# The first gate and up product of a transformer's FFN multiplied as a pair, with six slots of split weights and a ring of five

## The reference

```
mod = silu(c) @ ada_w + ada_b;  sh1, sc1, g1, sh2, sc2, g2 = split(mod, 6)
h = rms_norm(x, norm1_g) * (1 + sc1) + sh1
proj = h @ w_in + b_in                 # u, lru_gate, q, k, v, mix_gates
merged = gate_lru * (y_lru @ w_lru_out) + gate_attn * (y_attn @ w_attn_out)
x = x + g1 * (merged @ w_o)
h2 = rms_norm(x, norm2_g) * (1 + sc2) + sh2
gate, up = split(h2 @ w_ffn_in, 2)     # w_ffn_in: 2048 x 2*5632
x = x + g2 * ((silu(gate) * up) @ w_ffn_out)
x = rms_norm(x, final_g)
```

## Time and profile before

| | |
|---|---|
| median of 3 runs | 2730.45 us (2726.79 to 2730.5) |
| profiled execution: its time, its span | 2728.78, 2727.0 us |
| granted TensorE clock, mean | 0.997 |
| PE busy | 2688.0 us (99%) |
| DVE, ACT, POOL busy | 1889.8 (69%), 1317.2 (48%), 30.2 us (1%) |
| moved | 598.60 MB, mean 220 GB/s |
| chain that ended last | PE 89%, DVE 4%, DMA 3%, ACT 2% |

### The profile page before, as it was taken

One profiled execution on the slowest core, in us unless ns is written; L12 is line 12 of the kernel. 1 busy time (PEld: TensorE's weight loads), 2 busy tenths in 40 slices (PEclk: granted clock), 3 DMA queues, 4 the chain that ended last, 5 costly groups with the idle time before them and its releaser, 6 DMA issues.

```text
span 2727.0 us, 34023 instructions
## 1 busy us (share of the span) xinstructions
PE 2688.0 (99%) x13322; PEld 2258.8 (83%) x13322; DVE 1889.8 (69%) x2563; ACT 1317.2 (48%) x1874; POOL 30.2 (1%) x60
## 2 busy tenths in 40 slices
PE   8999999999999999999999999999999999999998
PEld 5888888888888788888888888888888888888886
DVE  7868777778886665554554477778587757765775
ACT  4158665544444644344434456554465434443443
POOL 0100000000000000000000000000000000000000
PEclk9999999999999999999999999999999999999999
DMA  9964657799987786555555555543555555555553
GB/s 363 409 256 155 220 198 262 266 344 351 329 278 235 232 271 215 194 191 192 186 193 191 194 181 187 176 146 133 197 196 188 192 193 186 190 193 194 188 191 125
DMA packets 161832, 598.60 MB, mean 220 GB/s; under 512 B 18151, under 2 KB 18376, under 8 KB 160392
## 3 DMA queue, kind: packets, MB, share of 16 engines
q1 hardware_dynamic: 154824, 564.71, 61.1%
q0 software_dynamic: 6848, 31.72, 3.0%
HBM read 592.17 MB, written 4.19 MB: 219 GB/s over the span
## 4 chain that ended last, share of the span: by engine, by line
PE 89%; DVE 4%; DMA 3%; ACT 2%; issue 1%; POOL 0%; SPq 0%; DVEq 0%; ACTq 0%
PE PS L681 88%; DMA W<-in_ada_first 2%; DVE ACC L1966 1%; DVE WL L1963 1%; DMA W<-in_w_mix 1%; ACT WH L1320 1%; PE PS L902 0%; PE PS L1099 0%; DMA W<-in_ada 0%; DVE G L1963 0%; DVE XB L1963 0%; DVE TT L1963 0%; DVE G L1966 0%; DMA W<-in_w_lru_out 0%; ACT L1546 0%
## 5 line engine op out<-in xcount | busy, mean ns | idle before, releaser
L1963 DVE TENSOR_TENSOR WL<-W,WH 128x1024 fp32r<-128x1024 f32 x876 | 1068.5, 1223 | 639.1 <-ACT WH L1320 637.6
L1320 ACT ACTIVATE WH<-W 128x1024 fp32r<-128x1024 f32 x876 | 924.5, 1058 | 818.5 <-PE PS L681 742.8
L681 PE MATMUL PS<-XA,WH 128*128 128x512 f32 x2480 | 799.6, 399 | 2.3 <-DVE WL L1963 1.6
L681 PE MATMUL PS<-WH,XA 128*128 128x512 f32 (+1 forms) x2560 | 797.1, 390 | 4.7 <-DVE XA L1963 4.3
L681 PE MATMUL PS<-WH,XB 128*128 128x512 f32 x1952 | 611.7, 391 | 0.0
L681 PEld LDWEIGHTS PS<-WH,XA 128*128 128x128 f32 x2560 | 479.3, 188 | 104.8 <-DVE XA L1963 5.9
L681 PEld LDWEIGHTS PS<-XA,WL 128*128 128x128 f32 x2480 | 466.2, 188 | 106.5 <-issue 0.7
L681 PE MATMUL PS<-WL,XA 128*128 128x512 f32 (+1 forms) x1280 | 495.7, 387 | 0.0
L681 PE MATMUL PS<-XA,WL 128*128 128x256 f32 x2480 | 491.8, 278 | 0.0
L681 PEld LDWEIGHTS PS<-WH,XB 128*128 128x128 f32 x1952 | 366.4, 188 | 76.1 <-issue 0.7
L681 PEld LDWEIGHTS PS<-XA,WH 128*128 128x128 f32 x2480 | 384.8, 189 | 6.1 <-DVE WL L1963 2.7
(11 more groups left out here) (231 smaller groups left out, 1333.6 us busy)
## 6 DMA issues: line engine op xcount, KB each, us to landing
W<-in_w_ffn_in SPq DMA_DIRECT2D x176, 512.0 KB, 4.2
W<-in_w_up SPq DMA_DIRECT2D x176, 512.0 KB, 3.8
W<-in_w_in SPq DMA_DIRECT2D x132, 512.0 KB, 4.2
W<-in_ada SPq DMA_DIRECT2D x128, 512.0 KB, 5.4
W<-in_w_ffn_out SPq DMA_DIRECT2D x88, 512.0 KB, 3.7
W<-in_w_down SPq DMA_DIRECT2D x88, 512.0 KB, 3.6
W<-in_ada_first SPq DMA_DIRECT2D x64, 512.0 KB, 9.2
W<-in_w_mix SPq DMA_DIRECT2D x64, 512.0 KB, 5.5
```

Of the source, the lines that this page charges most:

```text
L681: return e.matmul(o, l, r, start=start, stop=stop, skip_group_check=True)
L1320: return e.activation(o, a, ACT.Copy)
L1963: return e.tensor_tensor(o, a, b, op)
```

## The change

- `PAIR` = ("fg", 0) and ("fu", 0), multiplied by the new `moving_pair`: token half 0 of k tiles 0 to 3 for the one and then for the other, with the turn of token half 1 after the second k tile of the other; then token half 1 of the four for each; then k tiles 4 to 7 of the one, 4 to 7 of the other, and so on. `ring_plan` loads the weights in this order.
- USLOTS 4 to 6, RING 6 to 5 (12 raw slots at the start instead of 8). The two take 12 KB more of each partition, and the scratch for GpSimd's descriptors is cut from 16384 to 4096 bytes.
- ScalarE does the conversions of rest[0] and rest[1] before the first copies; VectorE does the one of rest[1] after the scaling of token half 1, and splits the residual of half 1 in two steps between the low parts. Both have one conversion for each of k tiles 4 to 15 then. ScalarE does two of the pair's conversions after the Silu of ("fg", 0).

```
-RING = 6
-USLOTS = 4
+RING = 5
+USLOTS = 6
...
         for h in c[::4]:
-            w += [("w_ffn_in", a + h + i) for a in (0, NHID) for i in range(4)]
+            if h == 0:
+                w += [("w_ffn_in", a + i) for i in range(4) for a in (0, NHID)]
+            else:
+                w += [("w_ffn_in", a + h + i) for a in (0, NHID) for i in range(4)]
...
+        def moving_pair(keys, X, name, turn_half, make):
...
             held = []
+            for key in keys:
+                free_bank(key)
+                for kt in range(EARLY):
+                    w.wait_ge(*xl[name, kt, 0])
+                    held += tiles(key, [kt])
+                    _, _, whi, wlo, _ = held[-1]
+                    three(key, X, kt, 0, whi, wlo, kt == 0, False)
+                    if key == keys[1] and kt == EARLY // 2 - 1:
+                        for j in range(EARLY // 2):
+                            turn_half(j, 1)
+            for n, (kt, key, whi, wlo, names) in enumerate(held):
                 w.wait_ge(*xl[name, kt])
+                m = three(key, X, kt, 1, whi, wlo, kt == 0, False)
                 if names:
                     m.then_inc(*mm(*names))
+                if n in (1, 3):
+                    make("begin", EARLY + n - 1)
+            for k in range(EARLY, KT, EARLY):
+                for key in keys:
+                    for kt in range(k, k + EARLY):
...
+                        three(key, X, kt, 0, whi, wlo, False, last)
+                        m = three(key, X, kt, 1, whi, wlo, False, last)
...
+                        if key == keys[0] and kt % 2 and kt + 3 < KT:
+                            make("begin", kt + 3)
...  scalar
         boundary(rest[0])
-        h2_half(0, (0, 1))
         boundary(rest[1])
-        h2_half(0, (2, 3))
+        h2_half(0, range(EARLY))
...
-        group([("fg", 0)], modulated, EARLY)
+        for i, u in enumerate(BEGIN[PAIR[0]][:PAIR_STEPS]):
+            if EARLY + i < KT:
+                modulated("begin", EARLY + i)
+            boundary(u)
...
+                if c == 0:
+                    for u in BEGIN[PAIR[0]][PAIR_STEPS:]:
+                        boundary(u)
...  vector
         boundary(rest[0])
-        h2_low(0, (0, 1))
-        residual(key, 3, ROW1, (1,))
-        boundary(rest[1])
+        h2_low(0, (0,))
+        gated(key, 3, ROW1, 1)
+        h2_low(0, (1,))
+        gated_in(key, 3, (1,))
+        h2_low(0, (2, 3))
         add_parts("r1", 1)
-        h2_low(0, (2, 3))
         invert("r1", 1)
         w.wait_ge(*iv["r1", 1])
         share(0, 1)
+        boundary(rest[1])
         shares(1)
         h2_low(1, (0, 1))
         boundary(rest[2])
         h2_low(1, (2, 3))
...
-    nc = bacc.Bacc("TRN2", target_bir_lowering=False, num_devices=1)
+    nc = bacc.Bacc("TRN2", target_bir_lowering=False, num_devices=1, dynamic_dma_scratch_size=4096)
```

More of the change, by code:

```diff
@@ L258 @@
 EARLY = 4
-GROUPS = [[("u", o) for o in range(NU)], [("gg", 0), ("gu", 0), ("gg", 1), ("gu", 1)]]
+PAIR = [("fg", 0), ("fu", 0)]
+PAIR_STEPS = 14
+GROUPS = [[("u", o) for o in range(NU)], PAIR, [("gg", 0), ("gu", 0), ("gg", 1), ("gu", 1)]]
 IN_GROUP = {k for g in GROUPS for k in g}
@@ L794, in moving, with tiles @@
                     between(i)
-        def moving_ramp(key, X, name, turn_half, make):
+        def moving_pair(keys, X, name, turn_half, make):
+            def tiles(key, kts):
+                return [(kt, key, *columns(width(key))) for kt in kts]
             held = []
[L799 to L811, removed]
-                w.wait_ge(*xl[name, kt])
[L813 to L819, removed]
@@ L820, in moving_ramp @@
                 if names:
                     m.then_inc(*mm(*names))
+                if n in (1, 3):
[3 more added lines that the diff above has]
+                    for kt in range(k, k + EARLY):
+                        w.wait_ge(*xl[name, kt])
+                        last = kt == KT - 1
+                        _, _, whi, wlo, names = tiles(key, [kt])[0]
+                        three(key, X, kt, 0, whi, wlo, False, last)
+                        m = three(key, X, kt, 1, whi, wlo, False, last)
+                        names += [key] if last else []
+                        if names:
+                            m.then_inc(*mm(*names))
+                        if key == keys[0] and kt % 2 and kt + 3 < KT:
+                            make("begin", kt + 3)
@@ L1110, in tensor @@
             for c in HIDDEN[ci]:
[L1111 to L1114, removed]
+                if c == 0:
+                    moving_pair(PAIR, XA, "h2", turn_half, second_norm)
+                    continue
+                moving(("fg", c), XA, ALLK, fourth=(lambda: f_turn(c - 1)) if c != HIDDEN[ci].start else None)
                 moving(("fu", c), XA, ALLK)
@@ L2350, in vector, with gated, gated_in @@
             soon.add(mg_low(n))
[L2352 to L2356, removed]
+        def gated(key, n, row, tb):
+            w.wait_ge(*(mm[key] if tb else mm[key, "half"]))
+            b = bank_of(key, tb)
+            tt(b, b, row[:, chunk(n)], ALU.mult).then_inc(*ev((key, "gated", tb)))
+        def gated_in(key, n, tbs):
             w.wait_ge(*rs.last())
@@ L2361, in residual @@
                    ALU.add).then_inc(*rs(*([key, (key, tb)] if tb else [(key, tb)])))
+        def residual(key, n, row):
+            w.wait_ge(*mm[key])
+            for tb in range(2):
+                gated(key, n, row, tb)
+            gated_in(key, n, (0, 1))
         w.wait_ge(*xs["x", 1, 1])
@@ L2389, in vector @@
         units(key, True, slice(-3))
-        residual(key, 3, ROW1, (0,))
+        gated(key, 3, ROW1, 0)
+        gated_in(key, 3, (0,))
         add_parts("r1", 0)
@@ L2420, in modulated @@
                 tt(XA[i][:, S:2 * S], TEMP["h2", i], XA[i][:, 0:S].bitcast(F32), ALU.subtract).then_inc(*xl(("h2", i)))
-        group([("fg", 0)], modulated, EARLY)
+        for i, u in enumerate(BEGIN[PAIR[0]]):
+            if EARLY + i < KT:
+                modulated("begin", EARLY + i)
+                modulated("end", EARLY + i)
+            boundary(u)
         def first_out(n):
```

## The result

| | before | changed |
|---|---|---|
| median (6 runs each, same chip) | 2729.74 us | 2739.98 us (2738.03 to 2742.84) |
| profiled execution: time, span | 2728.78, 2727.0 | 2740.47, 2738.7 |
| granted TensorE clock, mean | 0.997 | 0.996 |

The ratio is 1.0039, with an interval of 1.003 to 1.0049: slower by 10 us. 2726.7 was forecast, with 2733.0 as the upper end, so forecast and range both missed. What happened is rival (c) of the prediction, twice as large as it was priced.

The account below looks back on a forecast made before the run. TensorE was taken as the bound, busy 2688.0 of 2727.0 us. The terms, -3.2 - 1.5 + 1.3 + 0.5 = -2.9, from a middle of 2729.6 gave 2726.7 us, range 2721.5 to 2733.

Parts of the forecast that it names:

- rival (c): Merge stage, 575 to 700 us: the ring of five starves it, +9 us at 10% less pace, 2735.5 us; chance 0.13.
- Term 4: Merge stage, 600 to 650 us: five buffers just hold the pace, +0.5 us; bounds 0 and +7.
- The signs named for (c): Several TensorE waits for WL between 600 and 700 us, with less than 366 GB/s.
- The lead: Merge stage: ring and slots together hold eleven units instead of ten, 2.7 us more before a slower pace shows.
- Term 2: Six slots: the four waits for WL, the longest at 394.86 us, go; -1.5 us, bounds -1.9 and 0.
- Term 3: Start: one buffer less is one entry less in hand, so later entries land later; +1.3 us, bounds 0 and +3.
- Term 1: The pair, near 890 us: waits for XA fall from 4.33 to about 1.1 us; -3.2 us, bounds -4.3 and 0.
- The scratch: GpSimd's smaller descriptor space: no row known that prices it, taken as 0 with 1 us to either side.
- rival (a): The ring doesn't bind, only the pair and the slots count: 5 to 6 us less, 2724 us; chance 0.25.

Follow-up runs that it names:

- e1: The kernel before with five ring buffers instead of six and nothing else (four slots, scratch 16384): 2745.92 us, ratio 1.0064.
- e2: The kernel before with five ring buffers, six slots and scratch 4096, without the pair: 2745.53 us, ratio 1.0065.
- e6: The changed kernel, but from unit 112 to unit 240 ScalarE and VectorE split four units ahead instead of six: 2736.02 us, ratio 1.0025.
- e3: The kernel before with a scratch of 4096 and nothing else: 2728.37 us, ratio 0.9998.
- e7: The changed kernel with part of the ada weights brought forward from the merge stage: 2728.2 us, ratio 0.999.
- e11: The kernel before, six buffers, but transfers held as if there were five from unit 112 to unit 240: 2743.46 us, ratio 1.0051.
- e5: The kernel before with seven ring buffers, five slots and scratch 4096, without the pair: 2719.95 us, ratio 0.9965.
- e8: The kernel before with nine ring buffers, four slots and scratch 4096, without the pair: 2721.36 us, ratio 0.9967.
- e9: The changed kernel with seven buffers, five slots and two of the pair's conversions moved: 2715.55 us, ratio 0.9951.

## Why the prediction was wrong

- **Term 4, the merge stage: +0.5 forecast, +18.9 measured. This is the step that failed.** It held that five come round in 8.6 us, that landing and bare work are 8.1, and "so the pace can just be held". 8.6 is what came (1.72 x 5), but the pace needed was not that of 600 to 650 us. Over 620 to 713 us the six buffers had run at one entry per 1.54 us, and five at that pace would have had to come round in 7.7. And a buffer's time outside its landing never was the bare work: it contains the queues of ScalarE and VectorE, 3.2 us with six buffers and still 2.9 with five. Nor was 1.72 us the pace of those 50 us: it counts the 29 issues, while queue q1 moved 15.90 MB in them, 30.3 entries, so one per 1.65 us.
- The bound of that term took the pace down by a sixth over 50 us, and rival (c) by 10% over 125 us less 2.7. The 10% were right for the worst window. The length was wrong: all 200 us from 550 to 750 run slower, by 6 to 10%, together 15.2 us. The signs named for (c) came: five waits for WL between 676 and 694 us, and 338 GB/s for 366. The waits for G at 598.69 and for TT at 748.88 came where no term had one.
- **The lead did not count.** "Now they are eleven, 2.7 us more" was taken off both (c) and term 4. Slots only hold what the ring has brought. The earlier trace rows had the sign: a wait of 0.27 us at 650.73 means that the lead was already used up and that TensorE was moving at about the ring's pace (seven and nine buffers make the stage only 1.1 us shorter), so each per cent of pace was to be paid nearly in full. Instead it was read as a margin just sufficient. e1 and e2 show that the two slots bring nothing through this stage. Term 2 argued that "no engine waits longer for a slot"; it left out that the engines wait in their queues for a landing two units further ahead, which is the wait for TT (5.3 us, and 0.7 in e6).
- **The clock** after the two long gaps, 3.8 us, stood in no term.
- Term 3, five buffers at the start: +1.3 forecast with bounds of 0 and +3, +2.6 measured. The mechanism was right in the main: about one entry less by 62 us, as the sum has it, and 400 for 410 GB/s after, which it left to the bound. But the 355 GB/s from 53 to 62 us were not a full ring, since five buffers have 411 there. The seventh slab's sum, whose wait ended at 126.14, now starts at 127.9 without a wait (127.4 was foretold), but the eighth then waits until 142.82. The five kernels with five buffers stand at +1.6 to +3.3, those with six at 0, -2.1 and -1.8, so the kernel before was itself at the late end of its kind, and by the middle values the sixth buffer is worth some 4 us here.
- Term 1, the pair: -3.2 forecast, -4.4 measured, at its lower bound of -4.3. None of the small waits came that were laid out as 0.4, 0.2 and 0.5 us. What the forecast did not see is that the old waits can cost clock as well (last section).
- Term 2, six slots: -1.5 forecast. The waits near 395 went as told, -2.2 by the shift between 369 and 408 us, and the merge stage took it all back. The prediction priced the slots alone, as if nothing behind them could erase a gain.
- The scratch: 0 with 1 to either side; in the profiled executions the end is 2.2 us shorter, while e3's median is 1.2 us lower with a ratio of 0.9998.
- The sum of the parts: 18.8 - 4.4 - 0.6 - 2.2 = 11.6 us, beside a span that is 11.7 longer. Without the merge stage the change would have been 7 us faster, more than rival (a) thought.

## What to carry to other kernels

A ring's pace is its buffers divided by the time of one round, and the round holds the queues of the engines that empty it, not only landing and bare work; take both from the busiest stretch, and before a buffer is given away ask whether the consumer already waits there, however little, since then each per cent of pace is paid in full over the whole length of the stage. Lead in a later store (slots) is no lead unless the earlier store fills it: the same memory was worth 19.6 us more as seven buffers and five slots than as five and six. And loading that is not urgent, like the ada weights, can be moved out of the tight stretch for nothing but a line of numbers (11.8 us in e7), as long as the stage that takes it has room.

## What was not expected of the hardware

- **Equal gaps, unequal clocks.** The ramp of the kernel before and of e3 is the same code with the same gaps to within 0.6 us. Windows of 890 to 900 us, before and e3:

```profile
890.00:900.00 10.00, 7.54 (x39) 5.86 (x40) 6.30 (x15) 8.64 (x18) 0.00 (x0) 1.00 0.60 218
```

```profile
890.00:900.00 10.00, 8.31 (x32) 6.43 (x31) 4.98 (x11) 7.84 (x17) 0.00 (x0) 0.70 0.43 153
```

In e3 the granted clock is 0.70 there, a part of the window at 1.2 GHz instead of 2.4, and the ramp takes 2.1 us longer; in e1 likewise (0.73 from 910 to 920 us, and 2.3 us), in e11 less (0.83, 1.2 us). In the executions of before, e2, e5 and e8 it stayed at 1.00. So this cluster of waits costs up to some 2 us more than its own length, in some executions; without it, as in the changed kernel and e9, there is nothing to lose. What decides it was not tried.
- **The end of the program follows the scratch.** From the start of the last group of out transfers to the end of the span: 9.9 us in the three kernels with 16384, 7.6 in the nine with 4096, 6.5 with 2048, and 7.5 with 1024, where the last transfer is issued late. The same eight transfers of 256 KB land in 2.6 to 2.7 us (median) with each scratch, so it is not the transfers. Where it is spent lies outside what the profile shows.
